# Forgetting attention: the last four gate results leave the projection and are made by quarters in the attention's first 16 steps, their sigmoid built from the exponential

## The chip, the cores and the metric

The kernel runs on one core of a Trainium2 chip. The metric is the time of one execution on the device in microseconds (us), lower is better. The figure for a kernel is the median of its runs.

## The reference, cut to what matters

The program computes two stacks of transformer layers on 256 tokens of width 1024. The first stack and most of the second are untouched. The second stack has four layers on 272 tokens (16 meta tokens ahead of the 256); layers 0 and 3 mix their tokens by "forgetting" attention:

```python
def fox_mixer(h, w_in, b_f, q_gain, k_gain, w_out):     # H = 16 heads of 64
    q, k, v, gate, f = jnp.split(h @ w_in, [D, 2*D, 3*D, 4*D], axis=-1)
    q, k = rmsnorm per head of q (times 64 ** -0.5) and of k
    c = cumsum(log_sigmoid(f + b_f))                     # per head
    s = q @ k.T + c[query] - c[key], causal mask
    o = softmax(s) @ v
    return (o * sigmoid(gate)) @ w_out
```

The excerpt is shortened to its shape. The gate is a full 1024-wide result per token, and it is needed only where the attention's output is multiplied by its sigmoid, ahead of the output projection. All products are in float32.

## The kernel before, in words

**Stages.** Each of the core's engines walks the same list of stages. A mixer of this kind is three of them: `FoxProject` (normalisation and input projection), `CausalAttention`, and `AddProject` (times gate, output projection, addition to X). `FoxProject` and `CausalAttention` are divided by a barrier: TensorE, ScalarE and VectorE each drain and wait for the other two. `AddProject` flows on from the attention without one.

**Projection.** Tokens lie on the free axis (272, or 256 in the last layer where the meta tokens' queries and gates aren't needed). `w_in` is read in 16 slots of 256 columns (1 MB each) into a ring of six. Each weight slot is split into a high and a low part (ScalarE `upper`, VectorE `lower`), and so is the normalised input (`x_parts`, in the memory called H). A slot gives two results of 128 features: `product(pe, i, ...)` is 8 chunks of contraction x 3 matmuls (high-high, high-low, low-high), 24 matmuls for one result in one PSUM bank. The 32 results are, in this order: 8 of K, 8 of Q, 8 of V (slots 8 to 11, items 16 to 23) and 8 of the gate (slots 12 to 15, items 24 to 31). A gate result is moved by VectorE (times the inverse root, `by_root`, L4693) and then goes through a sigmoid in place on ScalarE (`in_place`, L4716). The loops over the results stop `LATER` items before the end, a number that is 0 here and 4 in `GdnProject`.

**Attention.** An item is a pair of heads with one tile of 128 queries: with 144 keys for the first tile, 272 for the second. The first layer has four more items, each of four heads ("quad") with the 16 meta queries: 20 items, against 16 in the last layer. The items go through a pipeline that is written out by steps; each engine runs its own list in this order:

- TensorE, step s: scores of item s; transposes of item s-3 (`due(step, 2)`); outputs of item s-4 (`due(step, 3)`).
- VectorE, step s: the two maxima of item s (L1087, which also applies the mask); reciprocal of the sums and weights of item s-2 (L1103, L1106, L1109); then `second_vector`, the copy of the second head's transposes of item s-3 out of PSUM (L1059); then `ahead_vector`.
- ScalarE, step s: the two exponentials of item s (L1144); the copy of the first head's transposes of item s-3 (L1157); the copy of the outputs of item s-4 (L1166); then `ahead_scalar`.

The transposes of an item wait for its weights and for the copies of the transposes before it in the same bank. The copies wait for the outputs that read the previous copy. `ahead_scalar` and `ahead_vector` do the output projection's preparation: the weight splits of its first slots (at steps N-7, N-4 and N-1 on ScalarE, N being the number of items) and, per finished chunk of 128 features, the product with the gate (`split_times`, L2967) and the two parts of it (L2972, L2976). PSUM bank 6 and bank 7 hold the outputs in turn; the exponentials `p` and the masked scores `s` lie in H.

## Time and profile before

| what | value |
|---|---|
| runs of the kernel | 2802.7, 2805.93, 2806.27 us; median 2805.93 |
| the profiled execution's own time | 2796.55 us |
| its span, first to last instruction | 2794.8 us |
| granted TensorE clock, mean over the span | 0.967 of full |
| busy share of the span | TensorE 93%, VectorE 69%, ScalarE 54% |

The profile is one execution with times per instruction. TensorE's matmuls overlap: one of 272 columns is shown with 0.29 us, while the next starts some 0.125 us later, so a stream of them is read by its starts. "Idle before" is the time that an engine stood still ahead of an instruction, with the instruction that released it. The clock is granted at one of two levels, 2.4 GHz (1.0 in the rows) and 1.2 GHz; a figure between is a stretch with both. The first attention runs from 1299.9 us to 1358.9, the second from 2531.9 to 2577.4.

### The profile page before, as it was taken

To read this page: it belongs to the slowest core of one execution; us is meant where nothing else is said; L and a number is where in the kernel's file an instruction comes from. 1 tells how busy PE (TensorE), PEld (TensorE's weight loads), DVE (VectorE), ACT (ScalarE), POOL (GpSimd) and SP (SyncE) were. 2 spreads that over 40 slices of the span, in tenths; PEclk is the share of its full clock that TensorE was granted. 3 is DMA by queue.
4 is the path that set the end of the run, shared out by engine and by line. 5 is a ranking of instruction groups with operands and counts; after the bars stand their busy time and mean duration, and the time that the engine had idled before them with its cause. 6 is when DMAs were issued, how large, how long until landed. Compare 5 with 4: busy or idle time off the path is not lost.

```text
span 2794.8 us, 54974 instructions
## 1 busy us (share of the span) xinstructions
PE 2599.9 (93%) x21006; PEld 2300.8 (82%) x21006; DVE 1929.9 (69%) x3491; ACT 1503.6 (54%) x2559; POOL 142.0 (5%) x180
## 2 busy tenths in 40 slices
PE   7988889997987999899899988999988899998999
PEld 5845678886776888698799988999877899997999
DVE  3167489997357999765667774777853577766677
ACT  3256378886356888654533464434742533455442
POOL 0010011100001111100000020000010000000000
PEclk9999989999998999999999999999978999999999
DMA  9281389997417999743255433555510355541553
GB/s 325 94 298 61 140 290 381 375 374 276 151 61 265 360 363 362 261 136 106 71 171 179 152 122 106 166 175 159 183 60 26 129 180 172 160 137 63 179 184 117
DMA packets 286594, 529.04 MB, mean 189 GB/s; under 512 B 14336, under 2 KB 207152, under 8 KB 285888
## 3 DMA queue, kind: packets, MB, share of 16 engines
q1 hardware_dynamic: 275472, 506.06, 52.3%
q0 software_dynamic: 9216, 12.61, 1.4%
q10 hardware_dynamic: 1712, 7.69, 0.7%
q8 instruction: 134, 2.20, 0.3%
q14 instruction: 60, 0.49, 0.1%
HBM read 526.21 MB, written 21.06 MB: 196 GB/s over the span
## 4 chain that ended last, share of the span: by engine, by line
PE 76%; DVE 7%; ACT 5%; issue 3%; DMA 1%; DVEq 0%; PEldq 0%; ACTq 0%; SPq 0%; PEld 0%; POOLq 0%
PE ps L2536 16%; PE ps L3119 6%; PE ps L3120 6%; PE ps L3121 6%; PE ps L2138 4%; PE ps L2139 4%; PE ps L2140 4%; PE ps L3139 3%; PE ps L3141 3%; PE ps L3140 3%; PE ps L2174 2%; PE ps L2175 2%; PE ps L2176 2%; PE ps L618 2%; DVE W_lo L2509 1%
## 5 line engine op out<-in xcount | busy, mean ns | idle before, releaser
L2536 PE MATMUL ps<-H_part,W_hi 128*128 128x272 f32 (+2 forms) x2052 | 458.7, 303 | 24.4 <-DVE H_part L2438 11.8
L2340 DVE TENSOR_TENSOR W_lo<-ring,W_hi 128x1024 fp32r<-128x1024 f32 x376 | 443.5, 1221 | 30.0 <-ACT W_hi L2259 29.0
L3168 ACT ACTIVATE W_hi<-ring 128x1024 fp32r<-128x1024 f32 x264 | 263.1, 1049 | 294.3 <-PE ps L3141 185.7
L3119 PE MATMUL ps<-room_part,W_hi 128*128 128x272 f32 (+1 forms) x1408 | 404.6, 287 | 5.0 <-DVE room_part L2438 5.0
L3120 PE MATMUL ps<-room_part,W_hi 128*128 128x272 f32 (+1 forms) x1408 | 403.4, 287 | 0.0
L3121 PE MATMUL ps<-room_part,W_lo 128*128 128x272 f32 (+1 forms) x1408 | 402.8, 286 | 0.0
L2259 ACT ACTIVATE W_hi<-ring 128x1024 fp32r<-128x1024 f32 x376 | 376.6, 1052 | 34.2 <-PE ps L2140 14.8
L2536 PEld LDWEIGHTS ps<-H_part,W_hi 128*128 128x128 f32 x2052 | 342.4, 192 | 42.5 <-issue 29.1
L2536 PE MATMUL ps<-H_part,W_lo 128*128 128x272 f32 (+2 forms) x1276 | 369.7, 299 | 2.1 <-issue 2.1
L3208 DVE TENSOR_TENSOR W_lo<-ring,W_hi 128x1024 fp32r<-128x1024 f32 x264 | 314.0, 1218 | 10.3 <-ACT W_hi L3168 9.4
L2509 DVE TENSOR_TENSOR W_lo<-ring,W_hi 128x1024 fp32r<-128x1024 f32 x182 | 219.8, 1247 | 116.6 <-ACT W_hi L2501 115.9
L3119 PEld LDWEIGHTS ps<-room_part,W_hi 128*128 128x128 f32 x1408 | 265.1, 188 | 7.8 <-issue 7.1
L3120 PEld LDWEIGHTS ps<-room_part,W_hi 128*128 128x128 f32 x1408 | 265.0, 188 | 0.1
L3121 PEld LDWEIGHTS ps<-room_part,W_lo 128*128 128x128 f32 x1408 | 265.1, 188 | 0.0
L3251 DVE TENSOR_TENSOR X<-X,ps 128x272 f32<-128x272 f32 (+1 forms) x352 | 139.2, 428 | 165.2 <-PE ps L3141 162.7
L2501 ACT ACTIVATE W_hi<-ring 128x1024 fp32r<-128x1024 f32 x182 | 181.8, 1051 | 124.3 <-PE ps L2536 86.5
L2536 PEld LDWEIGHTS ps<-H_part,W_lo 128*128 128x128 f32 x1276 | 242.0, 194 | 6.1 <-issue 2.2
L2138 PE MATMUL ps<-W_hi,A_split_hi 128*128 128x512 f32 x512 | 209.2, 409 | 3.6 <-DVE A_split_lo L2346 3.6
L3139 PE MATMUL ps<-room_part,W_hi 128*128 128x272 f32 (+1 forms) x704 | 201.7, 287 | 4.7 <-DVE X L3251 4.7
L2140 PE MATMUL ps<-W_hi,A_split_lo 128*128 128x512 f32 x512 | 202.5, 395 | 0.0
L2139 PE MATMUL ps<-W_lo,A_split_hi 128*128 128x512 f32 x512 | 202.4, 395 | 0.0
L3141 PE MATMUL ps<-room_part,W_lo 128*128 128x272 f32 (+1 forms) x704 | 202.0, 287 | 0.0
(627 smaller groups left out, 5119.4 us busy)
## 6 DMA issues: line engine op xcount, KB each, us to landing
ring<-in_w_expert SPq DMA_DIRECT2D x128, 1024.0 KB, 7.4
ring<-in_w_down SPq DMA_DIRECT2D x108, 1024.0 KB, 6.7
ring<-in_w_gate_up SPq DMA_DIRECT2D x88, 1024.0 KB, 5.1
ring<-in_w_mod SPq DMA_DIRECT2D x42, 1024.0 KB, 5.0
ring<-in_fox_w_in SPq DMA_DIRECT2D x32, 1024.0 KB, 5.8
ring<-in_gdn_w_in SPq DMA_DIRECT2D x16, 1024.0 KB, 5.9
ring<-in_gla_w_in SPq DMA_DIRECT2D x12, 1024.0 KB, 5.3
ring<-in_w_in_even SPq DMA_DIRECT2D x9, 1024.0 KB, 14.4
```

Source lines behind the costliest of these rows:

```text
L2138: pe.matmul(out, xh, wh[:, k, :], start=(q + k == 0), stop=False)
L2139: pe.matmul(out, xh, wl[:, k, :], start=False, stop=False)
L2140: mm = pe.matmul(out, xl, wh[:, k, :], start=False, stop=(q + k == KC - 1))
L2259: act.activation(self.parts(p)[0][:, W], c.ring[:, g % SLOTS, W], ACT.Copy).then_inc(c.hi_done, 1)
L2340: dve.tensor_tensor(lo, c.ring[:, (self.g0 + p) % SLOTS, W], hi.bitcast(F32), ALU.subtract)\
L2536: mm = pe.matmul(self.out(i), a, b, start=(k == 0 and n_part == 0), stop=(k == KC - 1 and n_part == 2))
L3119: pe.matmul(out, wh[:, k, M], hi, start=(k == 0), stop=False)
L3120: pe.matmul(out, wh[:, k, M], lo, start=False, stop=False)
L3121: mm = pe.matmul(out, wl[:, k, M], hi, start=False, stop=(k == KC - 1))
L3139: pe.matmul(out, wh[:, k, M], ah, start=(k == 0), stop=False)
L3141: mm = pe.matmul(out, wl[:, k, M], ah, start=False, stop=(k == 1))
L3208: dve.tensor_tensor(lo, c.ring[:, (self.g0 + p) % SLOTS, C], hi.bitcast(F32), ALU.subtract)\
```

## The change

The last four gate results (items 28 to 31, slots 14 and 15) are no longer made in `FoxProject`. Both their slots are still loaded and split there. In the attention, TensorE makes a quarter of a result (two chunks, six matmuls, PSUM bank 7) in each of the steps 0 to 15, between the transposes and the outputs. In steps 4, 8, 12 and 16 VectorE moves a finished one and ScalarE takes exp(-x); in steps 5, 9, 13 and 17 VectorE adds 1 and takes the reciprocal, ahead of `second_vector`. The attention's outputs now use two halves of bank 6, and an item's outputs wait for the copy of the item before it, not of the one before that. `x_parts` must live on in H, so `p` goes to the memory of K and `s` to another part of the room. The stop of the weight splits gets a number of its own (`UNSPLIT`), 2 in `GdnProject` as before.

```diff
@@ Attention.tensor
+            self.gate_tensor(pe, step)
             for i in self.due(step, 3):
...
-                if i >= 2:
-                    pe.wait_ge(self.scalar_done, self.act.at("out", i - 2))
+                if i >= self.OUTS:
+                    pe.wait_ge(self.scalar_done, self.act.at("out", i - self.OUTS))
@@ Attention.vector
+            self.gate_vector(dve, step)
             self.second_vector(dve, step)
@@ Attention.scalar
                 ins.then_inc(self.scalar_done, self.act.mark("out", i))
+            self.gate_scalar(act, step)
@@ class CausalAttention
+    OUTS = 1
+    def out_ps(self, i):
+        return self.c.ps[:, 6, P * (i % 2):P * (i % 2) + P]
+    def gate_tensor(self, pe, step):
+        if step < 16:
+            j, quarter = divmod(step, 4)
+            if j and not quarter:
+                pe.wait_ge(*self.project.moved(self.first + j - 1))
+            self.project.product(pe, self.first + j, 0, range(2 * quarter, 2 * quarter + 2))
+    def gate_vector(self, dve, step):
+        j, quarter = divmod(step - 4, 4)
+        if 0 <= j < 4 and quarter == 0:
+            self.project.move_vector(dve, self.first + j)
+        if 0 <= j < 4 and quarter == 1:
+            g = self.gates[j]
+            dve.wait_ge(self.scalar_done, self.act.at("gate", j))
+            dve.tensor_scalar(g, g, 1.0, None, ALU.add).then_inc(...)
+            dve.wait_ge(self.vector_done, self.dve.at("gate plus", j))
+            dve.reciprocal(g, g).then_inc(self.vector_done, self.dve.mark("gate", j))
+    def gate_scalar(self, act, step):
+        j, quarter = divmod(step - 4, 4)
+        if 0 <= j < 4 and quarter == 0:
+            act.wait_ge(*self.project.moved(self.first + j))
+            act.activation(self.gates[j], self.gates[j], ACT.Exp, scale=-1.0).then_inc(...)
+    def ahead_vector(self, dve, step):
+        for k in range(4, KC):
+            if step == self.done(k) + 4 + self.lag():
+                dve.wait_ge(self.vector_done, self.dve.at("gate", k - 4))
+        super().ahead_vector(dve, step)
@@ class FoxProject
+    LATER = 4
+    def out(self, i):
+        return super().out(i) if i < len(self.items) - self.LATER else self.c.ps[:, 7, 0:self.items[i][5]]
@@ class Stream, move_scalar and move_vector
-        ... and s + SPLIT_SLOTS < len(self.sources) - self.LATER // 2:
+        ... and s + SPLIT_SLOTS < len(self.sources) - self.UNSPLIT:
@@ fox
-    m["p"], m["s"] = (spare[:, 2048 * u:2048 * u + 6 * T2].rearrange("p (b t) -> p b t", b=6) for u in range(2))
+    m["p"], m["s"] = K[:, 0:6, :], c.room[:, 13824:13824 + 6 * T2].rearrange("p (b t) -> p b t", b=6)
...
-                     + normed_features(c, m["G"], range(12, 16), first, T2 - first, then=in_place(ACT.Sigmoid)),
+                     + normed_features(c, m["G"], range(12, 14), first, T2 - first, then=in_place(ACT.Sigmoid))
+                     + normed_features(c, m["G"][:, 4:8], range(14, 16), first, T2 - first),
```

## Rows read from the trace of the kernel before

**Rows 1.** The page: the chain that ended last, by engine; its costliest group.
```profile
PE 76%; DVE 7%; ACT 5%; issue 3%; DMA 1%; DVEq 0%; PEldq 0%; ACTq 0%; SPq 0%; PEld 0%; POOLq 0%
...
L2536 PE MATMUL ps<-H_part,W_hi 128*128 128x272 f32 (+2 forms) x2052 | 458.7, 303 | 24.4 <-DVE H_part L2438 11.8
```

**Rows 2.** Windows, the two attentions: length, busy by engine, clock, DMA share, GB/s.
```profile
1300.00:1358.90 58.90, 47.71 (x468) 35.13 (x469) 39.65 (x167) 38.18 (x138) 0.00 (x0) 0.89 0.06 19
...
2531.80:2577.40 45.60, 37.23 (x369) 26.88 (x369) 35.24 (x146) 32.80 (x110) 0.00 (x0) 1.00 0.08 25
```

**Rows 3.** Timeline of VectorE (start, us), two gate moves in each projection.
```profile
1286.83 0.44 DVE L4693 TENSOR_TENSOR room<-ps,stat 128x272 f32<-128x272 f32 x1 [1.43 <-PE ps L2536]
1289.84 0.44 DVE L4693 TENSOR_TENSOR room<-ps,stat 128x272 f32<-128x272 f32 x1 [2.57 <-PE ps L2536]
...
2522.43 0.42 DVE L4693 TENSOR_TENSOR room<-ps,stat 128x256 f32<-128x256 f32 x1 [2.40 <-PE ps L2536]
2525.26 0.42 DVE L4693 TENSOR_TENSOR room<-ps,stat 128x256 f32<-128x256 f32 x1 [2.40 <-PE ps L2536]
```

**Rows 4.** Timeline of TensorE, first attention: scores 0, transposes 0, scores 5, scores 16.
```profile
1299.86 0.52 PE L998 MATMUL ps<-ACC,room 64*128 64x144 f32 x4 [1.02 <-ACTq L4863]
...
1305.76 1.12 PE L1015 MATMUL ps<-small,H 128*128 128x128 f32 x4 [1.08 <-DVE H L1106]
...
1311.44 0.60 PE L998 MATMUL ps<-ACC,room 64*128 64x144 f32 x4
...
1336.79 0.73 PE L998 MATMUL ps<-ACC,room 64*128 64x272 f32 x4
```

**Rows 5.** Windows of the first attention's start and end (the clock follows POOL).
```profile
1305.70:1312.00 6.30, 6.24 (x33) 4.32 (x34) 3.29 (x17) 3.32 (x14) 0.00 (x0) 0.53 0.00 0
...
1352.00:1362.50 10.50, 9.43 (x52) 8.06 (x53) 5.59 (x12) 2.73 (x11) 0.00 (x0) 0.53 0.01 2
```

**Rows 6.** Timeline of TensorE, second attention: scores 5, steps 6 and 7, transposes 13.
```profile
2539.95 0.73 PE L998 MATMUL ps<-ACC,room 64*128 64x272 f32 x4
...
2542.46 0.52 PE L998 MATMUL ps<-ACC,room 64*128 64x144 f32 x4
...
2543.36 0.85 PE L1015 MATMUL ps<-small,H 128*128 128x128 f32 x6
2544.13 0.66 PE L1032 MATMUL ps<-room 128*64 128x128 f32 x8
2544.72 0.73 PE L998 MATMUL ps<-ACC,room 64*128 64x272 f32 x4
...
2545.84 0.66 PE L1015 MATMUL ps<-small,H 128*128 128x128 f32 x4
2546.43 0.88 PE L1032 MATMUL ps<-room 128*64 128x128 f32 x12
2547.23 0.52 PE L998 MATMUL ps<-ACC,room 64*128 64x144 f32 x4
...
2569.54 0.85 PE L1015 MATMUL ps<-small,H 128*128 128x128 f32 x6 [1.22 <-DVE room L1059]
```

**Rows 7.** VectorE: groups by shape, one reciprocal's line, one maximum of the timeline.
```profile
L1087 DVE CUSTOM_DVE_ANT_0 H<-ps,room 128x272 f32<-128x272 f32 x16 | 6.4, 438 | 4.7 <-PE ps L998 4.6
...
L1106 DVE TENSOR_SCALAR H<-H,room 128x272 f32<-128x272 f32 x8 | 2.9, 362 | 0.3
...
L1067 DVE MEMSET H<- 128x1632 f32 x1 | 1.4, 1418 | 0.9 <-ACTq L4863 0.9
...
L2470 DVE RECIPROCAL stat<-stat x8: 1752/1853/1854, 1194.0 to 2609.7; 128x272 f32<-128x272 f32 x7, 128x256 f32<-128x256 f32 x1
...
2546.08 0.44 DVE L1087 CUSTOM_DVE_ANT_0 H<-ps,room 128x272 f32<-128x272 f32 x1 [0.61 <-PE ps L998]
```

**Rows 8.** Timeline of ScalarE, second attention: an exponential, and a weight split.
```profile
2546.59 0.52 ACT L1144 ACTIVATE H<-H,room 128x272 f32<-128x272 f32 x1 [0.55 <-DVE room L1087]
...
2552.81 1.99 ACT L2501 ACTIVATE W_hi<-ring 128x1024 fp32r<-128x1024 f32 x2
```

## What I expect, before the changed kernel is run

> **What bounds the kernel now.** First the chain that ended last: TensorE holds 76% of it, and the costliest group is the projection's product line L2536 [rows 1]. The change touches two of the four second-stack mixers, so next come the windows of their attentions [rows 2]: 58.9 and 45.6 us long, with TensorE busy 47.7 and 37.2. The question is whether that idle time is in the places where the gate quarters are put. I then read the timelines: VectorE at the end of both projections, where its moves wait for nothing but TensorE's next result [rows 3], TensorE at the start of the first attention [rows 4], the granted clock there and at its end [rows 5], and TensorE through one steady pair of steps of the second [rows 6]. The reader should see that the idle time is at the start and the end of an attention, and that in the middle the eight-matmul groups follow one another almost without a gap.
>
> **What is removed.** A gate product is 24 matmuls. VectorE's moves of successive results stand 3.01 us apart in the first projection and 2.83 in the second [rows 3], which is TensorE's pace (125 and 118 ns a matmul). The stages end after a barrier: the last move, the sigmoid, then the attention's first scores. Results 28 to 31 are like 24 to 27, so the same tail (1.02 us idle, [rows 4]) now follows result 27, and what is removed is whole: 4 x 3.01 = 12.0 us and 4 x 2.83 = 11.3 us. The splits of the last two weight slots stay in the projection and end before result 27 does; nothing waits for them. Slots 14 and 15 are released during the attention instead of before it. The output projection's four loads wait for slots 10 to 13 (six slots of ring), so only the next stage's first two loads come later, and they are needed behind the output projection, a whole attention away: nothing. The splits of the output projection's slots 1 and 2 wait for gates 29 and 31, which are made by steps 7 and 15; the splits stand at steps 12 and 15 or later: nothing.
>
> **What is added on TensorE.** 16 quarters of six matmuls an attention: 0.75 us each in the first, 0.71 in the second. I follow the steps by their own work. From one pair of steps [rows 6]: scores of 144 keys 0.70 us (eight starts 87 ns apart), of 272 keys 1.12; transposes 0.49 and 0.77; outputs 0.59 and 0.80. That is 4.47 of the 4.77 us that the pair takes: two gaps, 0.2 and 0.1.
>
> *Start of the second attention.* Before, scores 5 begin 8.1 us after scores 0. With a quarter after each scores group, scores 3 end at about 5.5 instead of 3.8; its maxima, exponentials (2 x 0.5 us, [rows 8]) and ScalarE's copy of the first transposes follow, so the second transposes start at 7.9 instead of 6.7, then quarter, outputs, and scores 5 at 9.9. Five quarters (3.6 us) cost 1.8.
>
> *Start of the first.* Scores 5 come 11.6 us after scores 0 [rows 4]. VectorE first clears p (1.42 us, [rows 7]) and makes masks, and the first transposes wait for the exponentials, so they stay at 5.9 [rows 4]; quarters 0 to 2 go free into the waits. There the clock also falls: 0.53 granted from 1305.7 to 1312 [rows 5], the lower level of 1.2 GHz, after TensorE had stood idle for most of 6 us. With the waits filled I take it that it stays at 2.4; then scores 5 come at 10.6: a gain of 1.0 us.
>
> *Steps 5 to 15, first.* Scores, transposes and outputs at the durations above sum to 22.6 us of the 25.35 that the stretch takes (to scores 16, [rows 4]); the five-step period has two groups of four short heads, counted with 0.4, 0.2 and 0.9. Now 22.6 + 11 x 0.752 = 30.9, and 1.0 for gaps that no work fills (waits looked at in each step), plus VectorE's stalls below, 1.7: 33.6, that is +8.2.
>
> *Steps 5 to 15, second.* Own work 24.8 of 29.6 us (to transposes 13, [rows 6]; the 4.8 of gaps are mostly ScalarE behind after a 2 us weight split [rows 8], and TensorE that is later anyway lets it catch up). Now 24.8 + 7.8 + 1.1 + stalls 3.3 + 0.5 left of the last gap = 37.5: +7.9.
>
> **What is added on VectorE and ScalarE.** A gate costs VectorE a move (0.44, [rows 3]), an addition (0.36 by the tensor_scalar row, [rows 7]) and a reciprocal of 128x272, 1.85 us, of 128x256, 1.75 [rows 7]; starts stand about 0.1 closer than durations, so addition and reciprocal take some 2.1 us at one point, steps 5, 9, 13 and 17. They stand ahead of the copy of the second head's transposes in VectorE's queue. TensorE's next transposes wait for that copy. In a step with 272 keys VectorE needs from the end of the scores: maxima 0.73 (two of 0.44, overlapped), reciprocal 0.2, weights 0.56, then 2.1, then the copy 0.4: it is ready at 4.1 us. TensorE needs 0.49 + 0.71 + 0.80 and the next scores 0.70: 2.7 us. The difference is 1.4, less the first head's transposes (0.3), which don't wait for VectorE: 1.1 us a gate. In the second attention all four fall on such steps: 3.3 for the three inside the stretch. In the first, step 5 is followed by a quad item that ScalarE copies (0), step 9 is the same case before a quad item (1.4), step 13 has 144 keys (0.3): 1.7. The fourth gate's reciprocal, at step 17, has no quarter beside it: VectorE was idle 1.1 to 1.3 us near there, so 0.9 and 0.8 stay. VectorE needs about 4.15 of 4.77 us a pair now (idle 0.61, [rows 7]), then 10.8 a gate period of four steps against TensorE's 11.8: it does not become the bound, it only comes in a lump. ScalarE's exponential replaces a sigmoid of the same size, its table is the attention's own, and it has slack.
>
> **The other edits.** One output half-bank at a time (OUTS 1): outputs of i wait for ScalarE's copy of i-1, 0.27 us, which stands one instruction behind a copy that TensorE waits for anyway; beside scores and transposes of 1 us or more it costs nothing; without that cover, in 12 tail steps, at most 3 us (0.27 each), and I take 0.3. p and s in other memory: same instructions, nothing. The gate factors are awaited before the product with them: ready two steps earlier.
>
> **The sum.** First: -12.0 - 1.0 + 8.2 + 0.9 + 0.2 = -3.7. Second: -11.3 + 1.8 + 7.9 + 0.8 + 0.1 = -0.7. Together -4.4 us. The profiled execution took 2796.55 us (span 2794.8 and 1.75 around it), so its successor 2792.1; it lies 9.4 us under the median of the runs shown, 2805.93, so I forecast the median at 2801.5.
>
> The Trainium skill (TensorE: Matmul & The Clock Gate, Back-to-back issue gap) gives an isolated 272-column matmul 115.8 ns, and says that in pairs with weight loads the spacing is set by both. The row has 125 ns in such pairs. By the isolated figure the eleven quarters of the first attention would be 7.6 us instead of 8.3 and the sum lower by 0.6; I keep the row.
>
> **Rivals.**
> *A, the lump does not reach TensorE.* If the copies' wait for TensorE's own outputs covers the reciprocals (for it: TensorE is the later engine in every step with a quarter; against: the 4.1 against 2.7 above), the stalls 1.7 + 3.3 + 0.9 + 0.8 = 6.7 us go, and the time is 11.1 below: 2794.8.
> *B, slower: the lump costs its full size.* If each of the eight reciprocals also puts VectorE behind for the next step's maxima and exponentials, it costs 2.1 us instead of the 0.84 mean above: 8 x 1.3 = +10, the sum is +5.7: 2811.6. It decides from 1.4 us a gate on (8 x 0.55 = 4.4). For it: VectorE is busy 87% of a steady pair; against: with a quarter in each step TensorE gives it 1.1 us more a pair, time to catch up.
> *C, the clock.* In the first attention's last 10 us the clock also fell (0.53, [rows 5]), across the start of the output projection. If it now stays up the time falls by a further 3.5 us (half of about 7 us of work): 2798. If on the other hand the second attention's end, with a longer idle stretch at steps 17 to 19, or the first one's start loses it, that costs 3 to 5: 2805. The skill (same page, Part 1, What's actually happening) says that the throttled state is the default and that activity releases it; by that more work in the waits speaks for the first branch at the start, and [rows 5] agree in that the clock falls at a start full of waits.
> *D, no saving at the start.* The quarters wait for nothing, but stand before the next scores: if the start costs what it costs in work (3.8 and 3.6 instead of -1.0 and +1.8) the sum is +2.2: 2808.
>
> **How the numbers follow.** Forecast as above, between -9 and +1: 0.52, of it 0.12 below -5.6. A 0.20, C up 0.10, C down 0.06, D 0.05, B 0.07. Differences within 0.2% (5.6 us, about what a measurement of this kernel tells from none) count as the same: faster 0.12 + 0.20 + 0.08 = 0.40, slower 0.08, same 0.52. The range reaches to A with a little clock (-15: 2791) and to D and most of B (+4.5: 2810.5), leaving out about 0.15.
>
> **What the profile would show.** Right: both projection stages shorter by 12.0 and 11.3 us; TensorE with quarters of 0.75 and 0.71 us between transposes and outputs; attentions longer by about 8 and 10.5; four waits of TensorE for a VectorE copy of 1 us or more in the second attention, right behind the 1.75 us reciprocals; the granted clock at the first attention's start at full. Wrong: if the second attention grows by under 8 us the lumps are hidden (A); if by over 13, B. The forecast would fail altogether if the gate work were to be met by gaps in the middle that I counted as work.

## The result, and the profile after

| what | before | after |
|---|---|---|
| median of the runs made side by side | 2805.68 us (17 runs) | 2813.38 us (17 runs) |
| ratio, with its 95% interval | | 1.003 (1.0019 to 1.0041) |
| profiled execution's span | 2794.8 us | 2811.6 us |
| first attention, scores 0 to the first output product | 59.05 us | 73.76 us |
| second attention, the same | 45.53 us | 62.71 us |

The changed kernel is slower, by 0.3% or 7.7 us. The prediction, 2801.5 us with a range of 2791 to 2810.5, missed in sign and in range. Rival B gave 2811.6; whether for the right reason is settled below.

Both projections are shorter by what was forecast. The quickest way to see that is ScalarE's timeline. The table load for the first gate sigmoid of a projection stands at the same work in every version, and so does the load behind the mixer's end, in the next normalisation. Between the two lies all that the change touches. The kernel before first, then the one after; the columns are start and duration in us:

```profile
1276.51 1.28 ACT L4716 ACT_TABLE_LOAD   x1
1393.12 1.28 ACT L2465 ACT_TABLE_LOAD   x1
2510.00 1.28 ACT L4716 ACT_TABLE_LOAD   x1
2607.93 1.28 ACT L2465 ACT_TABLE_LOAD   x1
```
```profile
1276.41 1.28 ACT L4773 ACT_TABLE_LOAD   x1
1394.61 1.28 ACT L2517 ACT_TABLE_LOAD   x1
2519.65 1.28 ACT L4773 ACT_TABLE_LOAD   x1
2624.78 1.28 ACT L2517 ACT_TABLE_LOAD   x1
```

116.61 us became 118.20 and 97.93 became 105.13. These differences, +1.59 and +7.20, are called the net of the first and of the second mixer from here on; their sum, +8.8, is what the two changed mixers took more in this profile. From the first load to scores 0 the first mixer became 12.05 us shorter (before, scores 0 is the first of [rows 4]) and the second 11.3, as forecast, so the attentions took more than that back. The other 8 us of the two spans' difference lie between the two changed mixers, in stages whose code is the same: there two profiles of the kernel before are 0.2 us apart, those of other versions lie from 4.2 us under to 8.9 us over it, and two profiles of one and the same version (filled_tail below) are 5.9 us apart. The spans are therefore no measure here; the nets and the ratios of many runs are.

The waits of TensorE in the second attention (total us, times, longest) say what came in. First after the change:

```profile
PE ps L1015 <- DVE room L1071: 3.5, 5, 0.9
PE ps L2588 <- DVE room L4750: 3.0, 3, 1.2
PE ps L1015 <- ACT room L1170: 2.0, 3, 1.0
```

The second row is a wait that the prediction does not have: the gate product (L2588) waiting for VectorE's move of a gate result (L4750). The first attention has the same row:

```profile
PE ps L1015 <- ACT room L1170: 3.7, 4, 1.7
PE ps L2588 <- DVE room L4750: 3.3, 3, 1.2
```

TensorE's timeline of step 8 in the second attention (start, duration, idle before and who ended it):

```profile
2552.79 0.86 PE L1015 MATMUL ps<-small,room 128*128 128x128 f32 x6
2554.81 0.51 PE L2588 MATMUL ps<-H_part,W_hi 128*128 128x256 f32 x2 [1.16 <-DVE room L4750]
```

and VectorE's for the same moment:

```profile
2553.51 0.30 DVE L1099 CUSTOM_DVE_ANT_0 room<-ps,room 128x144 f32<-128x144 f32 x1
...
2553.93 0.29 DVE L1118 TENSOR_SCALAR room<-room 128x144 f32<-128x144 f32 x1
2554.14 0.29 DVE L1121 TENSOR_SCALAR room<-room 128x144 f32<-128x144 f32 x1
2554.34 0.42 DVE L4750 TENSOR_TENSOR room<-ps,stat 128x256 f32<-128x256 f32 x1
```

All four gate results share PSUM bank 7. In step 8 the first quarter of the third result may not be written before VectorE has moved the second, and that move stands late in VectorE's step 8: behind the maxima, which wait for this step's scores, and behind the weights. The reader is to see that VectorE was never idle here: it did this other work first. The matmuls that the move needs had ended in the step before.

The lumps that the prediction did name are there too, in steps behind a reciprocal, somewhat under the forecast size: 0.87 against 1.1 us in the second attention, twice, and 1.14 against 1.4 once in the first. VectorE, then TensorE (the last line is that of the first attention):

```profile
2544.94 1.75 DVE L1251 RECIPROCAL room<-room 128x256 f32<-128x256 f32 x1
2546.61 0.36 DVE L1071 COPY room<-ps 128x256 f32<-128x256 f32 x1
```
```profile
2547.12 0.52 PE L1015 MATMUL ps<-small,room 128*128 128x128 f32 x3 [0.87 <-DVE room L1071]
...
1317.61 0.30 PE L1015 MATMUL ps<-small,room 128*128 128x128 f32 x1 [1.14 <-DVE room L1071]
```

And the clock. Windows of the kernel after: the first attention's first 12 us, 6 us of its middle and its last 18, the second's last 18 (length; busy of TensorE, weight loads, VectorE, ScalarE, GpSimd with counts; granted clock; DMA share; GB/s):

```profile
1287.71:1299.71 12.00, 10.88 (x100) 8.48 (x102) 7.52 (x36) 5.93 (x21) 0.00 (x0) 1.00 0.28 87
...
1323.71:1329.71 6.00, 4.83 (x31) 3.81 (x31) 2.48 (x13) 1.69 (x6) 0.00 (x0) 0.72 0.01 3
...
1343.47:1361.47 18.00, 12.54 (x90) 8.73 (x90) 10.76 (x31) 9.34 (x32) 0.00 (x0) 0.76 0.00 0
...
2575.20:2593.20 18.00, 13.70 (x107) 10.29 (x108) 13.57 (x39) 8.77 (x27) 0.00 (x0) 0.77 0.19 59
```

The start held the upper level, as forecast (0.72 before in the same 12 us). Both ends lost it in part; before, the first end had 0.82 and the second 1.00 [rows 2]. The middle of the first attention lost it too, from 36 us behind scores 0 on; the kernel before had 1.00 there. No term of the prediction has this fall.

### The profile page after: what moved, and what is told of

It is laid out like the page before. It is cut to its first block, busy times and chain, and to the rows that moved or that the text cites. A ratio compares the mean times of both kernels' runs of the same rounds, so it can differ in the third digit from the quotient of the medians.

```text
span 2811.6 us, 55006 instructions
## 1 busy us (share of the span) xinstructions
PE 2614.1 (93%) x21006; PEld 2309.8 (82%) x21006; DVE 1944.6 (69%) x3507; ACT 1506.0 (54%) x2559; POOL 141.4 (5%) x180
## 4 chain that ended last, share of the span: by engine, by line
PE 76%; DVE 7%; ACT 4%; issue 3%; DMA 1%; PEldq 0%; DVEq 0%; ACTq 0%; SPq 0%; PEld 0%; POOLq 0%
PE ps L2588 17%; PE ps L3176 6%; PE ps L3177 6%; PE ps L3178 6%; PE ps L2190 4%; PE ps L2192 4%; PE ps L2191 4%; PE ps L3196 3%; PE ps L3198 3%; PE ps L3197 3%; PE ps L2226 2%; PE ps L2227 2%; PE ps L2228 2%; PE ps L618 2%; DVE W_lo L2561 1%
## 5 line engine op out<-in xcount | busy, mean ns | idle before, releaser
L2588 PE MATMUL ps<-H_part,W_hi 128*128 128x272 f32 (+2 forms) x2052 | 466.8, 306 | 29.3 <-DVE H_part L2490 11.8
L2588 PEld LDWEIGHTS ps<-H_part,W_hi 128*128 128x128 f32 x2052 | 345.4, 193 | 50.0 <-issue 29.5
L2588 PE MATMUL ps<-H_part,W_lo 128*128 128x272 f32 (+2 forms) x1276 | 372.5, 302 | 0.8 <-issue 0.8
L3265 DVE TENSOR_TENSOR W_lo<-ring,W_hi 128x1024 fp32r<-128x1024 f32 x264 | 313.9, 1218 | 10.6 <-ACT W_hi L3225 10.0
L2588 PEld LDWEIGHTS ps<-H_part,W_lo 128*128 128x128 f32 x1276 | 245.1, 197 | 6.3 <-issue 2.5
```

The costliest lines, as they stand in the source:

```text
L2588: mm = pe.matmul(self.out(i), a, b, start=(k == 0 and n_part == 0), stop=(k == KC - 1 and n_part == 2))
L3265: dve.tensor_tensor(lo, c.ring[:, (self.g0 + p) % SLOTS, C], hi.bitcast(F32), ALU.subtract)\
```

## The experiments

"both" in the following is the version with both repairs; line numbers of the versions differ by a few. Times of attentions are again scores 0 to the first output product.

**outs_alone: the kernel before, with the outputs' two half banks.**
```diff
-                if i >= 2:
-                    pe.wait_ge(self.scalar_done, self.act.at("out", i - 2))
+                if i >= self.OUTS:                       # 1 in CausalAttention
+                    pe.wait_ge(self.scalar_done, self.act.at("out", i - self.OUTS))
```


> The kernel before, with one part of the change alone: the outputs use two halves of bank 6 and wait for the copy of the item before (OUTS 1). Nothing else moves. My theory (the shared bank is not where the time went): both attentions stay at 59.1 and 45.5 us from the first scores to the first product of the output projection, within 0.5 us each; time the same as before. Rival (the tighter bank is a main cost of the change): the attentions grow by 2 us or more each and the time by 0.15% or more.

Ratio 0.9994 (0.998 to 1.0009). First net +0.28: the term of 0.3 us was right. Second net +4.16, but not from this wait: TensorE's waits are those of before (the one for the outputs' copy 0.91 instead of 0.78 us), and the clock over the attention's last 18 us is 0.76 instead of 1.00. That is the subject of the last experiments.

**move_first: VectorE moves the finished gate result at the start of its step, ahead of the maxima.**
```diff
@@ Attention.vector, ahead of the maxima of step
+            self.gate_move(dve, step)      # move_vector, taken out of gate_vector
```


> The changed kernel, with VectorE's move of a finished gate result put at the head of its steps 4, 8, 12 and 16, ahead of the maxima and weights. My theory: the changed kernel has a wait that my prediction did not name: there is one PSUM bank for the gate results, so the first quarter of gates 1 to 3 (steps 4, 8, 12) waits for the move of the one before, which stands behind two maxima and two weights in VectorE's queue. TensorE's idle of 0.6 to 1.2 us in front of these quarters goes, six times in all: the attentions go from 73.8 to about 70.5 us and from 62.7 to about 59.5, the time is 6 to 7 us under the changed kernel's. Rival (TensorE meets VectorE's lag there, and would meet it at the next copy instead): the idle time moves to the transposes behind, and each attention changes by under 1 us.

Ratio 0.9991 (0.9978 to 1.0004), nets -3.04 and +0.97, attentions 68.17 and 57.51 us. The wait for the move is gone in the second attention, and one of 0.5 us is left of the 3.3 in the first. The clock at the second attention's end was at 1.00 in this profile, so the fair neighbour is after_again (below: +1.50 and +4.02, the same clock there). Against it the second mixer gains 3.05 us, which is the 3.0 us of its waits, and the first 4.5: 2.8 us of waits and 1.7 more. The clock's fall in the middle of the first attention is gone as well (1.00 in the same stretch), which may be a part of the 1.7.

**invert_late: addition and reciprocal go behind the copy of the transposes; the move stays.**
```diff
             self.second_vector(dve, step)
+            self.gate_invert(dve, step)    # the addition and the reciprocal
```


> The changed kernel, with the addition and the reciprocal put behind the copy of the second head's transposes, in the same steps 5, 9, 13 and 17; the move stays where it was. My theory (as predicted): the reciprocal costs TensorE some 0.9 us where it stands ahead of that copy, four times in the second attention and about twice in the first: 62.7 goes to about 59.5 and 73.8 to about 72, the time is about 5 us lower. Rival (VectorE is simply short of time for a step, and the lump delays the next step's maxima, exponentials and transposes by as much): under 1 us in each attention.

Ratio 1.0021 (1.0002 to 1.0039), nets +0.45 and +3.28. Still slower than before, with every wait for the move in place. Against after_again, with the second attention at full clock in both profiles, the place of the reciprocals is worth 1.1 and 0.7 us.

**both: the two together.**
```diff
+            self.gate_move(dve, step)      # ahead of the maxima
...
-            self.gate_vector(dve, step)
             self.second_vector(dve, step)
+            self.gate_vector(dve, step)
```


> The changed kernel with both: the move first in its step, addition and reciprocal behind the copy. If the two waits are separate and are the whole excess over what the quarters cost, the gains add up: first attention about 69 us, second about 56.5, and the time some 11 us under the changed kernel's, so a little under the kernel before. If they are two views of one shortage of VectorE, both together give hardly more than the better one alone. What is left over the prediction (67.1 and 56.1) would be the quarters themselves: in the second attention they take 0.88 us each from the start of the first matmul to the start of the next group, where I had taken 0.71.

Ratio 0.9981 (0.9966 to 0.9996), nets -3.10 and +0.27. Attentions 68.28 and 56.78 us, where the prediction's terms give 67.4 and 56.1 (the expectation above says 67.1). Beside the moved move, the place of the reciprocals is worth 0.1 and 0.7 us. VectorE's list now, around a gate's move:

```profile
2543.87 0.42 DVE L1074 COPY room<-ps 128x256 f32<-128x256 f32 x1 [0.95 <-PE ps L1033]
...
2544.87 0.42 DVE L4757 TENSOR_TENSOR room<-ps,stat 128x256 f32<-128x256 f32 x1
2545.21 0.30 DVE L1103 CUSTOM_DVE_ANT_0 room<-ps,room 128x144 f32<-128x144 f32 x1
```
and TensorE goes from the transposes into the quarter without a gap:
```profile
2544.39 0.86 PE L1015 MATMUL ps<-small,room 128*128 128x128 f32 x6
2545.35 0.51 PE L2595 MATMUL ps<-H_part,W_hi 128*128 128x256 f32 x2
```

**no_invert: both, without the reciprocals.** The gate factor stays 1 + exp(-x), so this kernel leaves out the inversion.
```diff
-            dve.reciprocal(g, g).then_inc(self.vector_done, self.dve.mark("gate", j))
```


> The kernel with both waits moved out of the way (move first, inversion behind the copy), without the eight reciprocals: the gate factor stays 1 + exp(-x), so the output is not the reference's. It prices what is left of the reciprocals. My theory after the last runs: their place in the queue is worth 0.7 us a stage or less, because VectorE catches up beside the quarters; without them the attentions go from 68.3 and 56.8 to about 67.3 and 55.3, some 2.5 us together. Rival (the forecast's term, stalls of 6.7 us in all, which only moved to other waits): 65.5 and 53.5 or less.

Ratio 0.9995 (0.998 to 1.001), nets -4.33 and -2.24. Against both, with nearly the same clock (0.74 and 0.71 over the first attention's last 18 us, 1.00 in the second), the eight reciprocals cost 1.2 and 2.5 us of the mixers: 3.7 us, or 0.47 each, of 1.75 to 1.85 us of their own. The ratio of the runs does not show it; its interval overlaps that of both.

**halves: both, two quarters in every second step.**
```diff
+            if quarter % 2 == 0:
+                self.project.product(pe, self.first + j, 0, range(2 * quarter, 2 * quarter + 4))
```


> The kernel with move first and inversion behind the copy, with each gate made in two halves of twelve matmuls (in the even steps) in place of four quarters. The same 96 matmuls an attention, half as many places. If a quarter costs more than its six matmuls at each entry and exit (0.88 us from its first start to the next group's, against 0.71), both attentions get shorter by up to 8 x 0.15 = 1.2 us. If that excess is only time taken over from the transposes ahead of it (these take 0.41 and 0.62 now, 0.49 and 0.77 before), nothing is gained, and a block of 1.5 us in one step may cost 0.5 to 1 us more in waits.

Ratio 1.0008 (0.9995 to 1.0021), nets -3.05 and +5.12. In the first mixer the cut makes no difference; in the second the clock was at 0.75 over the attention's last 18 us, where both had 1.00. Whether the cut did that, this run cannot tell (see the last experiments).

**one_gate and two_gates: both, with one and with two results moved.**
```diff
-    LATER = 4
+    LATER = 1        # 2 in two_gates
```


> The kernel with move first and inversion behind the copy, with only the last gate result moved: quarters in steps 0 to 3 alone, where TensorE waits for the pipeline to fill, one move and one reciprocal an attention. The projections get shorter by 3.0 and 2.8 us. My theory (quarters cost nothing in the first start and half in the second, and their full price from step 5 on): the attentions grow by 0 to 0.5 and 1 to 1.5 us, both mixers together 3.5 to 4.5 us under the kernel before, a little better than with four gates (2.8). Rival (the gain per gate is the same wherever it stands): a quarter of the four gates' gain, 0.7 us.

> The same with the last two gate results, quarters in steps 0 to 7. Projections 6.0 and 5.7 us shorter; the second gate's quarters stand in full steps and cost their 0.75 us less the gaps that they fill: attentions about +3 and +5 us. Together 3 to 4 us under the kernel before, no better than one gate. Rival (full steps have gaps enough for quarters): 6 us or more under it.

Ratios 1.0007 (0.9992 to 1.0022) and 0.9992 (0.9975 to 1.001). Nets -3.13 and +0.49, sum -2.64, for one; -2.99 and +0.39, sum -2.60, for two; both has -3.10, +0.27, -2.83. All three had nearly the same clock (1.00 at the first attention's start, some loss at its end, 1.00 through the second; two_gates also lost it for 6 us in the middle of the first). In the profiles one result has all the gain of four: in the steady middle a result costs what it saves, and the gain is made in the first attention's first steps, where its quarters also keep the clock up (1.00 over the first 12 us, 0.72 before). The ratios don't bear this out to the same degree: the one of both is the lowest, with intervals that just touch.

**after_again and before_again: the two kernels once more.**

> The changed kernel once more, for a second profile. It asks what of its excess repeats. The six waits for the gate bank (L2588 from L4750, 3.3 and 3.0 us) should be there to 0.1 us, since nothing in them is chance. The clock is the open part: in the first profile it fell once in the middle of the first attention and at the end of the second. If these falls belong to the changed kernel's waits they are there again (attentions 73 to 74 and 62 to 63 us); if they are chance, the second attention can be near 59 this time.

> The kernel before once more, for a second profile. With the outputs' bank alone changed, the second attention was 48.6 us with the same waits to 0.1 us and a clock that fell at its end; in the kernel before it was 45.5 at the full clock. If the clock there is chance, this profile may show either 45.5 or about 48.5; the first attention stays at 59 to 60. If it always shows 45.5, the fall belongs to the shared bank after all.

after_again: the move waits are the same (3.3 and 3.0 us), and so is the clock's fall in the middle of the first attention (0.72 over the same 6 us); nets +1.50 and +4.02; the second attention's clock stayed at 1.00, and its net is 3.2 us smaller than the first time. before_again: nets +0.07 and -0.01, with the clock as in the first profile. So 3.2 of the +8.8 us were the clock of that one execution.

**quarter_ahead: both, the quarter ahead of the transposes.**
```diff
+            self.gate_tensor(pe, step)      # ahead of the transposes
...
-            self.gate_tensor(pe, step)
             for i in self.due(step, 3):
```


> The kernel with move first and inversion behind the copy, with the quarter ahead of the transposes in each step, where TensorE waits for the copies, in place of behind them. My theory: TensorE's waits in the quarter steps are at the transposes (some 3.5 us from ScalarE's copy and 1.4 to 1.9 from VectorE's in each attention); a quarter of 0.75 us ahead of them uses that time: attentions 68.3 and 56.8 get about 2 us shorter each, the mixers together 6 to 7 us under the kernel before. Rival (the copies are late because the whole step is: TensorE's later transposes make weights and copies later, and the wait comes back at the outputs): under 0.5 us.

Ratio 1.0007 (0.9992 to 1.0023), nets -1.14 and +5.27: worse than both by 2.0 us in the first mixer, where the clock had about the same losses (0.74 and 0.71 over the last 18 us). In the second it was at 0.75 there, so that net says nothing of the order. The wait for the move is back, though VectorE makes the move first in its step. TensorE's waits in the first attention, then in the second:

```profile
PE ps L2595 <- DVE room L4757: 2.3, 2, 1.9
...
PE ps L2595 <- DVE room L4757: 2.4, 3, 1.0
```

In the version with both repairs it was 0.5 us in the first attention and none in the second. The quarter now comes so early in TensorE's step that the move, although first in VectorE's, is not done; behind the transposes it nearly always is. The 1.8 us more of this wait are near the 2.0 that the first mixer lost, but other waits became shorter and the clock fell in the middle of the attention too, so the loss is not divided between them.

**filled_tail: both, with six unread matmuls of 256 columns in every step from 17 on.** The results of these matmuls go into the gates' bank and nobody reads them.
```diff
+        elif step > 16:
+            if step == 17:
+                pe.wait_ge(*self.project.moved(self.first + 3))
+            high = self.project.parts[0]
+            for n in range(6):
+                pe.matmul(self.c.ps[:, 7, 0:256], high[0][:, 0:P], high[1][:, 0:256], start=True, stop=True)
```


> The kernel with move first and inversion behind the copy, with six matmuls of 256 columns into the free gate bank added in each step from 17 on, whose results nobody reads. It adds about 0.7 us of work to TensorE in each of the last steps (seven in the first attention, three in the second), where it waits for copies. If its clock falls at the end of the first attention because it stands idle there, it now stays at 2.4 GHz, and the first attention, at 68.3 us with 0.71 granted over its last 18 us, gets some 2 to 3 us shorter in spite of the work; the second, which had the full clock, gets 0 to 1.5 us longer. Rival (the work isn't free): both get longer, by up to 5 and 2 us.

Ratio 0.9975 (0.9964 to 0.9987), nets -5.25 and +0.65. The windows of the first attention's last 18 us and of the 5 us behind it, in both:

```profile
1338.08:1356.08 18.00, 12.99 (x93) 9.37 (x90) 10.94 (x33) 9.83 (x32) 0.00 (x0) 0.71 0.00 0
1356.08:1361.08 5.00, 5.00 (x28) 5.00 (x29) 4.22 (x5) 0.49 (x2) 0.00 (x0) 0.67 0.01 3
```
and in filled_tail:
```profile
1338.98:1356.98 18.00, 14.93 (x143) 11.94 (x143) 11.74 (x37) 10.61 (x33) 0.00 (x0) 1.00 0.00 1
1356.98:1361.98 5.00, 5.00 (x40) 5.00 (x41) 4.22 (x5) 0.49 (x2) 0.00 (x0) 1.00 0.00 0
```

In the first 5 us of the output projection TensorE starts 40 matmuls instead of 28. The waits of both in this stretch, and what became of them:

```profile
1339.88 0.63 PE L1015 MATMUL ps<-small,room 128*128 128x128 f32 x4 [1.67 <-ACT room L1174]
...
1345.68 0.40 PE L1015 MATMUL ps<-small,room 128*128 128x128 f32 x1 [1.85 <-DVE room L1119]
...
1354.28 1.55 PE L1033 MATMUL ps<-room 128*64 128x128 f32 x12 [0.91 <-ACT room L1183]
```
```profile
1341.44 0.63 PE L1015 MATMUL ps<-small,room 128*128 128x128 f32 x4 [0.96 <-ACT room L1174]
1341.82 0.95 PE L1250 MATMUL ps<-H_part 128*128 128x256 f32 x6
...
1347.63 0.30 PE L1015 MATMUL ps<-small,room 128*128 128x128 f32 x1 [0.83 <-DVE room L1119]
```

Useless work in the waits made the first mixer 2.15 us shorter than in the version with both repairs, because the useful matmuls beside and behind it ran at 2.4 GHz: 0.7 us of it in the attention, the rest in the output projection behind it. The ratios, 0.9975 here and 0.9981 for both, don't tell the two apart. The Trainium skill (TensorE: Matmul & The Clock Gate, A second HAM failure mode: psum-queue depth-cycling) tells of a kernel whose TensorE stood still for short times between groups and so went back and forth between the two levels. The trace without the unread matmuls agrees: no wait here is above 1.9 us, and the level changed in the middle of the stretch.

**filler_alone: no result moved; the unread matmuls in steps 0 to 3 and from 17 on.**
```diff
-    LATER = 4
+    LATER = 0
...
-        if step < 16:
+        if step < 4 * self.project.LATER:
...
+        elif step > 16 or step < 4:         # then as in filled_tail
```


> No gate result is moved at all: all sixteen stay in the projection with their Sigmoid. Kept are the half banks of the outputs, the new homes of p and s, and unread matmuls: six of 256 columns (0.88 us by the quarters' rows) in each of steps 0 to 3 and from step 17 on. It asks what a held clock alone is worth. Clock alone: before's first attention ran its first 12 us at 0.72 and its last 18 us at 0.82; at 1.00 that is some 3.4 us at the start and up to 3.2 at the end of the first attention less 4 us of unread matmuls in each pair of places, so -2 to -5 us for the two mixers, as good as the filled version that moves the gates (-4.6 net), and the whole gain there was the clock. Gates as well: if moving them is worth something of its own under a held clock, this version gains 0 to -1.5 us and the filled version with moved gates is better by 3 or more. Rival: the fillers cost their own time and buy nothing here (+3 to +8 us).

Ratio 1.0006 (0.999 to 1.0022), nets -2.60 and +3.75, the clock at 1.00 through both attentions. The second reading is the nearer one: this version loses 1.15 us in sum (it was to gain 0 to 1.5) where filled_tail gains 4.6. A held clock alone gives 2.6 us in the first mixer; in the second, where it was already up before, the fillers cost 3.8.

**first_only: four results moved in the first attention alone, with the fillers there; outputs in half banks in both.**
```diff
+    later = 4 if first == 0 else 0
...
+    project.LATER = later
```


> The four gate results are moved in the first attention only, with the unread matmuls from step 17 there; the second mixer keeps its projection and its attention of before apart from the half banks of the outputs. By the nets of the filled version (first mixer -5.25 us, second +0.65) the first mixer gives -5.3 us and the second 0 (up to +4 if the clock falls at its end, as it did once with the same waits): 2800.5 us, ratio 0.998, against 0.9975 for the filled version with both. If what the first mixer gained there was chance, its net is nearer the -3.1 us of the version without unread matmuls.

Ratio 0.9984 (0.9971 to 0.9996). First net -5.25, as before; second +5.43, with the second attention's code that of outs_alone.

**filled_again: filled_tail once more, on the chip of those two.**

> The filled version once more, on the same chip as the two above: 2799 us, ratio 0.9975, mixers -4.6 us, and the clock at 1.00 through both attentions again if the unread matmuls hold it. If it falls at the end of one of them, the first reading was luck, and the ratio is 0.998 to 1.000.

Ratio 0.9985 (0.9974 to 0.9996), nets -5.23 and +2.54. The first attention's clock was again 1.00 throughout; in the second, the last 18 us had 0.91, so the fillers do not hold it for certain there.

**first_pure: first_only, with two output banks in the second attention.**
```diff
+        self.OUTS = 1 if project.LATER else 2
...
+        return self.c.ps[:, 6, P * (i % 2):P * (i % 2) + P] if self.project.LATER else super().out_ps(i)
```


> As the version with four gates moved in the first attention only, and the second attention with its outputs in two banks again, as before the change: there its instructions and waits are those of the kernel before. First mixer -5.2 us, as in three profiles. Theory chance: the clock at the second attention's end falls in some executions whatever the outputs' banks, so it is at 1.00 or at 0.75 here, second mixer 0 to +5.4. Theory banks: the fall (0.77 and 0.75 over the last 18 us, in both profiles with half banks and without moved gates) comes with the half banks, and with two banks the clock stays at 1.00 and the second mixer is at 0 to +0.3. Ratio 0.998 for both, 0.9975 if the banks were it.

Ratio 0.9983 (0.997 to 0.9996), nets -5.26 and +4.09. **outs_again: outs_alone once more**, one profile:

> The kernel before with the outputs in half banks alone, once more. Theory banks: the clock falls again over the last 18 us of the second attention (0.77 the first time), second mixer +4. Theory chance: it may as well stay at 1.00, second mixer 0 to +0.5.

Nets +0.34 and +4.18. The last 18 us of the second attention in first_pure, then in outs_again:

```profile
2560.14:2578.14 18.00, 12.75 (x102) 9.26 (x103) 10.88 (x39) 9.84 (x32) 0.00 (x0) 0.77 0.00 0
```
```profile
2569.13:2587.13 18.00, 12.61 (x102) 9.12 (x103) 10.84 (x37) 9.80 (x32) 0.00 (x0) 0.77 0.00 1
```

The theory of the banks falls: with two banks, and with this attention's instructions those of before, the clock fell as well; TensorE's waits up to there agree with those of the kernel before within 0.02 us. The ratios say the same. If half banks lost the clock in every execution and two banks in none, outs_alone would be 4.4 us, or 0.16%, slower than the kernel before; its interval ends at 1.0009. Of the six profiles whose second attention has no gate work and no filler (before twice, outs_alone, outs_again, first_only, first_pure) two kept it and four lost it, for 4.1 to 5.4 us.

## Why the prediction was wrong

**The failed step.** "What is added on VectorE and ScalarE" counts the move as 0.44 us of VectorE's time and lists whom the new work delays: the copy behind it. It never asks who waits for the move. The diff has that wait in plain sight (`pe.wait_ge(*self.project.moved(self.first + j - 1))`), ahead of the first quarter of a result and of the outputs and the next scores behind it. In rival D I even wrote that "the quarters wait for nothing". The wait costs 6.3 us (3.3 and 3.0, three times in each attention, in both profiles of the changed kernel), and taking all but 0.5 us of it away while keeping all the work turned 1.003 into 0.9991. Put into the sum it turns the sign: -4.4 + 6.3 = +1.9.

**The rest of the miss** is in part the clock. In after_again, with the second attention at full clock, the sum of the nets is +5.5; in the first profile, where its end fell, +8.8. Between +1.9 and +5.5 lie the second attention's start (0.8 us more than forecast) and the 1.7 us by which the first mixer gained more from move_first than the 2.8 us of waits that went; 1.1 us are not assigned to anything. The clock's fall in the middle of the first attention goes with these 1.7 us: it is there in both profiles of the changed kernel and in invert_late (0.72 over 6 us), and not in move_first and both. That it costs them is not shown: halves and two_gates have a fall at the same place and the nets of both. The fall at the second attention's end had a branch in rival C, at 3 to 5 us and a chance of 6 in 100. It should have had more: the clock fell at the second attention's end in four of six profiles without gate work or fillers there.

**What was right.** With the missing wait removed, both gives what the prediction had worked out for the change: attentions of 68.28 and 56.78 us against 67.4 and 56.1, mixers -2.8 against -4.4. The forecast of +8 and +10.5 us for the attentions is nearly met by this version (9.2 and 11.3), not by the changed kernel (14.7 and 17.2, or 15.0 in after_again). The prediction's sign "by over 13, B" would have named the wrong cause here. By its steps:

- Projection, -12.0 and -11.3: measured 12.05 and 11.3.
- Start of the first attention at full clock: right. Scores 5 came 11.68 us after scores 0 with a move's wait of 0.92 in it, and 10.50 in the version with both repairs, against 10.6. Start of the second: 10.7 in that version, against 9.9; that is most of the second mixer's difference from the forecast (+0.27 against -0.7).
- Middle, by periods of four steps in the second attention, scores 5 to scores 9: forecast 11.8 + 1.1 = 12.9 us; 14.51 after the change, of it 1.16 the move's wait; 13.02 in the version with both repairs.
- The lump at the forecast place, 0.87 us against 1.1 and 1.14 against 1.4, but rarer: of the four waits of 1 us or more in the second attention two came, with 0.87. And its effect on the end is less than its size: moved behind the copy it gives back 0.8 us in all, left out altogether 3.7, against 6.7 in the sum (5.0 in the middle, 1.7 in the tail). So this term was too large: 6.7 us in the sum, 4.5 measured.
- Output half banks, 0.3: measured 0.28 and 0.34 in the first mixer.

**The rivals.** A (2794.8) falls: the reciprocals reach TensorE, since leaving them out takes 3.7 us off. B has nearly the measured time and the wrong reason, so its hit is luck: it wanted 2.1 us per reciprocal, and they cost 0.47 behind the copy and 0.1 to 0.2 more ahead of it. C's first branch did not come: the first attention's end lost the clock again (0.76 over its last 18 us, 0.82 before). Its second came in one profile of two, for 3.2 us, at the second attention's end; the first one's start stayed up, as the sum had it. D falls: it needed scores 5 at 15.4 and 11.7 us behind scores 0, and in the version with both repairs they came at 10.5 and 10.7.

**Where the gain of 23.3 us in the projections went.** It was never a gain but a move: in the middle of an attention TensorE has no idle time that fits six matmuls, so each quarter costs its length there. one_gate's nets show it from the other side: one result moved saves as much as four.

**A version that beats both kernels.** filled_tail has the lowest ratio, 0.9975, and 0.9985 the second time; first_only, first_pure and both lie at 0.9984, 0.9983 and 0.9981 with intervals that overlap. Which of them is best is not told apart. What can be said: all four are faster than the kernel before by 4 to 7 us; of the first mixer's 5.25 us, which came in four profiles within 0.03, 3.1 come with moved results alone (whose quarters also hold the clock at the start), 2.6 with unread matmuls alone; and in the second mixer moved results give nothing (+0.3 to +0.7 with the clock up).

**What stays open.** Why the clock falls at the second attention's end in some executions and not in others. Neither the banks nor the gate work decides it. That it hangs on when in time the stretch is reached would explain it, and is only argued.

## What to carry to other kernels

When a result's storage is shared by the next one, its move out is on the path of the engine that fills it: put the move first in the mover's step and the next writing late in the filler's, and go through every wait that a diff adds, one by one, asking what stands ahead of the instruction that ends it. Work moved into another stage is worth only the idle time that it finds there, so count those places first. And where TensorE loses the clock in a stretch of short waits, six unread matmuls a step can be cheaper than the waits; that must be measured place by place, since where the clock was already up they cost their own time.

## What the runs showed of the hardware that was not expected

- The same kernel keeps the clock in one execution and loses it in another: the changed one had 0.77 and 1.00 over the last 18 us of the second attention, 3.2 us of time. first_pure, with that attention's instructions and waits of before, had 0.77 against 1.00, for 4.1 us. One profile of each kernel is no ground for a difference of that size. Yet the fall in the middle of the first attention (0.72 over 6 us) came at the same place in both executions.
- TensorE's clock fell in stretches where no single wait was above 1.9 us (0.71 over 18 us), and six unread matmuls in each step from 17 on held it at 1.00 in five profiles of five in the first attention, and in two of three in the second.
- The mixers between the two changed ones, with unchanged code, differed by -4.2 to +8.9 us from the first profile of before, and by 5.9 between two profiles of one version. Both profiles of the changed kernel lie at the upper end (+8.2 and +8.9); whether that is chance is not shown, and the cause is open.
